# GpSimd in place of VectorE for the low part of the second weight unit of ff0 and ff1, in two halves

## What is computed

```
x = layer_norm(ALPHA * x + (1 + g1) * y, ln_g[l, 0], ln_b[l, 0])   # y: output of the mixer
h = x * (1 + sc2) + sh2                                            # sc2, sh2 from the conditioning vector
g, u = split(h @ w_ffn_in[l], 2);  y = (silu(g) * u) @ w_ffn_out[l]
```

## Time and profile before

| | |
|---|---|
| median of 3 runs | 1643.99 us (1643.86 to 1647.81) |
| the profiled execution | 1643.41 us, span of its instructions 1641.5 us |
| TensorE matmul busy | 1600.4 us, 97% |
| VectorE busy | 1082.9 us, 66% |
| ScalarE busy | 810.3 us, 49% |
| GpSimd busy | 230.4 us, 14% |
| low parts in halves on VectorE (line 1956) | 6, of 1218 ns each (ff0, ff1 and f1a) |
| stretch where ff0 begins | about 154 to 183 us |
| stretch where ff1 begins | about 481 to 505 us |

### The profile page before, as it was taken

One profiled execution on the slowest core, in us unless ns is written; L12 is line 12 of the kernel. 1 busy time (PEld: TensorE's weight loads), 2 busy tenths in 40 slices (PEclk: granted clock), 3 DMA queues, 4 the chain that ended last, 5 costly groups with the idle time before them and its releaser, 6 DMA issues.

```text
span 1641.5 us, 24504 instructions
## 1 busy us (share of the span) xinstructions
PE 1600.4 (97%) x9244; PEld 1336.9 (81%) x9244; DVE 1082.9 (66%) x1331; ACT 810.3 (49%) x1039; POOL 230.4 (14%) x309
## 2 busy tenths in 40 slices
PE   4999999999999999999999999999999999999999
PEld 2997888879877888788888978888888889888887
DVE  8798988889667556855547976455655547665544
ACT  2565533446555434654456665444544445664443
POOL 2002011000000000088853200000000003100000
PEclk9999999999999999999999999999999999999999
DMA  9976889775646655375554336665466555346552
GB/s 343 345 256 216 305 309 313 246 256 175 236 129 220 230 190 179 129 222 194 185 179 136 124 107 208 189 194 180 158 204 199 181 190 169 127 160 199 181 186 96
DMA packets 225912, 330.11 MB, mean 201 GB/s; under 512 B 10584, under 2 KB 187321, under 8 KB 225839
## 3 DMA queue, kind: packets, MB, share of 16 engines
q1 hardware_dynamic: 210496, 276.93, 51.5%
q0 software_dynamic: 14944, 52.06, 9.3%
q10 hardware_dynamic: 398, 0.11, 0.0%
HBM read 327.97 MB, written 1.09 MB: 200 GB/s over the span
## 4 chain that ended last, share of the span: by engine, by line
PE 83%; DVE 10%; ACT 3%; DMA 2%; issue 2%; SPq 0%; DVEq 0%; POOL 0%; ACTq 0%
PE bank L2891 41%; PE bank L2620 24%; PE bank L2608 7%; DVE s_wL L1946 2%; PE bank L2578 2%; PE bank L2903 2%; DVE s_late L1973 2%; DMA s_late<-in_w_ada 1%; PE bank L2590 1%; ACT s_wH L1493 1%; DVE s_late L1987 1%; PE bank L2730 1%; PE bank L2675 1%; DMA s_raw<-in_w_in_ab 1%; DVE s_mix L753 1%
## 5 line engine op out<-in xcount | busy, mean ns | idle before, releaser
L1946 DVE TENSOR_TENSOR s_wL<-s_raw,s_wH 128x2048 fp32r<-128x2048 f32 x251 | 580.4, 2313 | 293.7 <-ACT s_wH L1493 293.2
L1493 ACT ACTIVATE s_wH<-s_raw 128x2048 fp32r<-128x2048 f32 x254 | 485.2, 1911 | 205.0 <-PE bank L2891 157.6
L2891 PE MATMUL bank<-s_wH,s_hH 128*128 128x512 f32 x1056 | 420.2, 398 | 3.3 <-DVE s_hL L2343 2.9
L2891 PE MATMUL bank<-s_wH,s_hL 128*128 128x512 f32 x1056 | 412.1, 390 | 0.0
L2891 PE MATMUL bank<-s_wL,s_hH 128*128 128x512 f32 x1056 | 411.4, 390 | 0.0
L2891 PEld LDWEIGHTS bank<-s_wH,s_hH 128*128 128x128 f32 x1056 | 198.4, 188 | 47.5 <-issue 5.8
L2891 PEld LDWEIGHTS bank<-s_wH,s_hL 128*128 128x128 f32 x1056 | 198.2, 188 | 42.6
L2891 PEld LDWEIGHTS bank<-s_wL,s_hH 128*128 128x128 f32 x1056 | 198.6, 188 | 39.4 <-issue 0.5
L2620 PE MATMUL bank<-s_wH,s_aH 128*128 128x512 f32 x496 | 194.2, 392 | 1.3 <-ACT s_gate L1501 1.0
L2620 PE MATMUL bank<-s_wH,s_aL 128*128 128x512 f32 x496 | 193.3, 390 | 0.0
L2620 PE MATMUL bank<-s_wL,s_aH 128*128 128x512 f32 x496 | 193.0, 389 | 0.0
(11 more groups left out here) (467 smaller groups left out, 2247.4 us busy)
## 6 DMA issues: line engine op xcount, KB each, us to landing
s_raw<-in_w_ffn_in SPq DMA_DIRECT2D x88, 512.0 KB, 5.1
s_raw<-in_ffn_w_gate SPq DMA_DIRECT2D x88, 512.0 KB, 3.9
s_raw<-in_ffn_w_up SPq DMA_DIRECT2D x88, 512.0 KB, 4.9
s_raw<-in_ffn_w_down SPq DMA_DIRECT2D x88, 512.0 KB, 4.3
s_late<-in_w_ada POOLq DMA_DIRECT2D x11, 2048.0 KB, 10.7
s_raw<-in_w_ffn_out SPq DMA_DIRECT2D x44, 512.0 KB, 4.4
s_late<-in_w_ada POOLq DMA_DIRECT2D x18, 1024.0 KB, 5.7
s_raw<-in_w_in_ab SPq DMA_DIRECT2D x24, 512.0 KB, 9.0
```

The source lines that it names most:

```text
L1493: A(wH[:, slot, :], raw[:, slot, :], ACT.Copy).then_inc(hi_ready, 1)
L1946: TTn(wL[:, slot, :], raw[:, slot, :], wH[:, slot, :].bitcast(F32), ALU.subtract).then_inc(lo_ready, 1)
L2891: last = mm(bank[gu_bank(name, i, tt)][:], h, w[:, k, :], start=(half == 0 and k == 0 and j == 0), stop=(half == 1 and k == 3 and j == 2), ...
```

## The change

GpSimd gets a `split_quarters` of its own: two subtractions of 128 x 1024, with the same two semaphores. It is called in GpSimd's program in l = 0 behind `ada(0, 0, 5120, 32)` and ahead of the loop of `late_halves`, and in l = 1 behind `load_ln(1, 0)` and ahead of `ada(1, 0, 5632, 72)`. It waits for the high part of n0+1 and for the low parts of all units up to n0. VectorE leaves its two halves out for ff0 and ff1, and waits for `lo_ready` of n0+1 before it makes the low part of n0+2.

```
+        POOL_SPLITS = ("ff0", "ff1")
...
+            def split_quarters(n):
+
+                pool.wait_ge(hi_ready, n + 1)
+                pool.wait_ge(lo_ready, n + LO0)
+                for half, done in enumerate((ev("lo_half"), lo_ready)):
+                    at = slice(UNIT // 2 * half, UNIT // 2 * half + UNIT // 2)
+                    pool.tensor_tensor(wL[:, n % RING, at], raw[:, n % RING, at], wH[:, n % RING, at].bitcast(F32), ALU.subtract)\
+                        .then_inc(done, 1)
+
             for l in range(2):
                 pool.wait_ge(nat_ready, 2 * TR[("o_ab", "o_cd")[l]] + 2)
                 load_ln(l, 0)
                 if l == 1:
+                    split_quarters(START["ff1"] + 1)
                     ada(1, 0, 5632, 72)
                 if l == 0:
                     pool.dma_start(bias[:, 0:8, :], toep_tile(12, 8)).then_inc(toep_in, 16)
                     ada(0, 0, 5120, 32)
+                    split_quarters(START["ff0"] + 1)
                     with pool.Fori(0, 2) as m:
...
                 normalise(1)
-                if first:
+                if first and first not in POOL_SPLITS:
                     split_quarters(START[first] + 1)
...
                 lower_piece(name, 1, 1)
+                if name in POOL_SPLITS:
+                    dve.wait_ge(lo_ready, START[name] + (LO0 + 2))
                 split_py(START[name] + 2)
```

## The result

The changed kernel takes 1647.67 us, the median of 14 runs (1646.74 to 1648.22); the kernel before, in the same session, 1644.11 us (14 runs, 1643.4 to 1647.81). That is 3.56 us more, ratio 1.0019 [1.0012, 1.0026]. The forecast was 1644.3, the range up to 1647.2. The profiled execution took 1646.93 us (span 1645.2).

The account below looks back on a forecast made before the run. TensorE was taken to hold 83% of the chain, with VectorE's LayerNorm ahead of ff0 and ff1 exposed. Lock cost 1.15 less gain 0.82 gave +0.33 us on the 1643.99 median: 1644.3 us, range 1642.4 to 1647.2.

Parts of the forecast that it names:

- I take 1.9 us a half: Each GpSimd subtraction of 128x1024 was put at 1.9 us, with ends of 1.88 and 2.6 us.
- Second half 158.22 to 160.13: In ff0, GpSimd's second half follows VectorE's sum, which ends at 158.36 after starting 0.69 us late; chain 0.78 us late.
- The gain: Taking the halves off VectorE shortens TensorE's waits in ff0 and ff1: 0.41 us a layer, 0.82 us for both.
- the wait of 0.28: TensorE's wait for the first half, behind the transposes, goes: 0.28 us a layer.
- the third piece: The third piece of hL starts at 170.31 in place of 170.80 in ff0, gaining another 0.13 us a layer.
- Exposure: VectorE's LayerNorm lines 2291 and 2281 wait for GpSimd's halves, the PSUM line 2276 doesn't; cost 1.15 us for both layers.
- The lock costs nothing: Rival: the halves fall beside unexposed VectorE operations or gaps, only the 0.82 us gain remains: 1643.2 us; chance 0.22.
- By the loads: Rival: n0+4's load, requested 9.5 us early, takes bandwidth from n0+3 and TensorE waits in ff0: 1650.3 us; chance 0.03.
- TensorE's clock falls: Rival: longer waits ahead of ff0 and ff1 bring the clock to 1.2 GHz, 1.7 us each: 1647.7 us; chance 0.06.
- Doesn't do what it says: Rival: GpSimd comes too late or takes far longer, so TensorE waits for it, some 5 us a layer: 1653 us; chance 0.02.

Follow-up runs that it names:

- the kernel with the gap: Changed kernel, but GpSimd waits for its own first half before issuing the second: 1645.39 us, +0.75 over the kernel before, ratio 1.0005.
- nothing formed: Changed kernel, but GpSimd only raises the two semaphores and nobody makes those low parts: 1642.87 us, -1.77 against the kernel before, ratio 0.999.
- the fillers' kernel: Changed kernel with 19 TensorE filler matmuls in place of 5 ahead of ff0: 1648.77 us, +3.94 over the kernel before, ratio 1.0025.
- ff1_behind_dma: Changed kernel with ff1's ln_b load held until tile 0's second product, both halves directly behind it: 1651.65 us, +6.9 over the kernel before, ratio 1.0044.
- ff0_early: Changed kernel with ff0's two halves put ahead of GpSimd's loads of toep_scratch and conditioning weights: 1645.33 us, +0.58 over the kernel before, ratio 1.0002.
- ff1_later: Changed kernel where GpSimd's first half in ff1 also waits for tile 0's second product: 1647.7 us against 1644.51 for the kernel before, ratio 1.0019.

## Why the prediction was wrong

**The steps that failed.** Two, both in the cost of the addition.

"I take 1.9 us a half": it is 2.36 us (2.35 to 2.42), inside the ends given (1.88 to 2.6). The nearest row by shape had an fp32 output; this one writes fp32r, and no run separates that. The Trainium skill's figure (GPSIMD Engine Reference, section 3.1), 2.25 us a half by estimate, was the nearer one, and the measured 2.36 is above even that.

"Second half 158.22 to 160.13": this step took for granted that VectorE's waiting sum would be served when the first half ended, and that the second half would wait for it. In ff0 the second half went first. With 2.36 us and VectorE served in between, the steps give the sum some 1.15 us of waiting, near what the kernel with the gap measured (1.26, with line 2281 another 0.42 late). With both halves ahead it is 3.55. That is the loss by the traces: 3.11 us in ff0 for a forecast of 0.78 - 0.41 = 0.37, and 0.74 in ff1 for 0.37 - 0.41 = -0.04, less 0.7 regained behind ff0, 3.15 in all. The medians' 3.56 has 0.4 on top, for the most part from the groups of executions. The trace of before had the question in it: line 1450's 2.98 us shows GpSimd waiting behind VectorE, but in those rows each GpSimd operation waits for the one before it (it starts some 0.07 us behind its end); none has two issued back to back with a VectorE one waiting, and I read it as turn by turn, with no bound for the other order. Had I bounded it (both halves ahead of the sum: 2 x 1.9 - 1.1 = 2.7 us in ff0, and 2 x 2.6 - 1.1 = 4.1 at the upper end), the range would have held the result.

**ff1.** Sum 0.77 us late in place of 0.28, normalisation 0.42 in place of 0.09: 1.19 against 0.37, nearly all from the longer half.

**The gain was right.** 0.41 us a layer was forecast, from the wait of 0.28 and the third piece; with nothing formed the nets are -0.44 and -0.42. In the changed kernel's ff1, ScalarE's high part of 492.34 is 1.19 late beside 373 and that of 500.9 is 0.74: 0.45 gained in between.

**Exposure was right.** So was that a delay there goes one for one into the time: 3.55 us of waiting less 0.44 of gain is the net of 3.11. The product from PSUM is untouched beside GpSimd (0.67 us). Line 2281, which no row showed and I counted as exposed, is: 0.81 becomes 1.23 in ff1. By the Trainium skill (SBUF — State Buffer, "SBUF: two separate sides") the port pair that the two engines share is an exclusive lock, held for a whole instruction, also against a two-port operation; the runs agree (1.23, and 1.06 us of waiting for an 8-column operation). Of whose turn comes next, when one engine has a second instruction ready, it says nothing, and that was the larger part.

**The rivals.** *The lock costs nothing* is refuted by the 3.55 and 0.77 us of waiting. *By the loads*: n0+4's high part at 181.12 no longer waits for its transfer (in the kernel before it waited 1.82 us), and nothing waits for n0+3; the earlier load is harmless and worth nothing, as forecast. *TensorE's clock falls* came true as an event (0.71 and 0.50 in 164 to 168), and its forecast time, 1647.7, is the measured one, but that is chance: the fillers' kernel without the fall has the same net (+3.09), the longer falls in ff0 are worth 0.4 and 0.8 us at most, and the forecast had wanted the fall in both layers where only ff0 has it. Its price, 1.7 us for 3.4 us at half pace, came out nowhere in ff0. A rival whose number fits isn't thereby the cause. *Doesn't do what it says*: the halves are done at 161.1, and TensorE comes to them at 172.4.

## What to carry to other kernels

Work moved to GpSimd lands wherever VectorE's SBUF operations are, and each can wait for whatever GpSimd has issued: check the place of a piece, not only its length, and bound the case in which all pieces issued back to back go ahead of the waiting operation. A wait between the pieces bounded the damage here (1.95 us against 4.24), and placing the pieces between VectorE's SBUF operations brought ff0 down to +0.13; splitting finer without such placing only made the pieces meet more operations (nets +1.50 and +1.30). Before any of it, price the gain by leaving the work out: here it was 0.86 us in all, less than one lockout.

## What I had not expected of the hardware

- One VectorE operation can be passed over by two GpSimd operations in a row: 3.55 us in ff0, 3.88 us in ff1_behind_dma. Where the first of them started under a VectorE sum, the next sum lost 0.77 to 0.82 us only (the changed kernel's ff1, ff0_early, ff1_later). Which property of the start decides is open.
- A GpSimd subtraction to fp32r with nothing in its way takes 2.36 us for 1024 columns and 1.27 us for 512; by estimate from the two, some 0.2 us each time and 2.1 ns a column. The rows of 1.6 us for 512 and 2.8 us for 1024 contain a wait for VectorE.
- A fall of TensorE's granted clock behind a long pause cost nothing in ff0 where it lasted some 3.4 us (beside a chain that was late anyway), 0.4 and 0.8 us there where it lasted some 6.8, and 1.45 us in ff1_behind_dma's ff1, also for some 6.8.
- The fall at the turn near 365 us lasts 3.4 us in some executions and 6.8 in others of nearly the same program, worth roughly 0.6 to 1.2 us: two groups of times within a kernel that look like an effect of an edit.
